# First modulation of a two-layer mixer kernel: eight tiles of two k instead of four blocks of four

## The reference

```
shift, scale, gate = split(SiLU(cond) @ w_mod[l] + b_mod[l], 3)       # w_mod[l]: 2048 x 6144
xn   = rmsnorm(x, norm_w) * (1 + scale) + shift
proj = xn @ w_in[l]                                                   # 2048 -> 6176 columns
```

## Time and profile before

| | us |
|---|---|
| three executions | 2139.41, 2141.55, 2141.57 |
| the profiled execution | 2140.41 |
| its span, first to last instruction | 2138.6 |
| PE busy in the span | 2103.1 |
| VectorE busy | 1447.0 |
| ScalarE busy | 644.0 |

### The profile page before, as it was taken

One profiled execution on the slowest core, in us unless ns is written; L12 is line 12 of the kernel. 1 busy time (PEld: TensorE's weight loads), 2 busy tenths in 40 slices (PEclk: granted clock), 3 DMA queues, 4 the chain that ended last, 5 costly groups with the idle time before them and its releaser, 6 DMA issues.

```text
span 2138.6 us, 34996 instructions
## 1 busy us (share of the span) xinstructions
PE 2103.1 (98%) x13797; PEld 1894.9 (89%) x13797; DVE 1447.0 (68%) x2819; ACT 644.0 (30%) x1092; POOL 178.5 (8%) x118
## 2 busy tenths in 40 slices
PE   5999999999999999999999999999999999999998
PEld 4788887888999999999998888888799999999998
DVE  5869899999666656775465454566666566677654
ACT  4232221321333324442142222232133333353312
POOL 0000000000000000533310000000000000043321
PEclk9999999999999999999999999999999999999999
DMA  9989787675323324554435546454333233366443
GB/s 368 387 298 324 224 280 239 224 236 173 115 91 103 106 75 153 181 200 149 120 118 175 158 145 204 133 152 153 113 123 106 75 98 106 93 214 202 155 122 143
DMA packets 357333, 365.42 MB, mean 171 GB/s; under 512 B 17670, under 2 KB 264156, under 8 KB 356572
## 3 DMA queue, kind: packets, MB, share of 16 engines
q1 hardware_dynamic: 328528, 320.67, 46.8%
q10 hardware_dynamic: 28684, 43.09, 5.4%
HBM read 304.98 MB, written 58.72 MB: 170 GB/s over the span
## 4 chain that ended last, share of the span: by engine, by line
PE 95%; DMA 1%; DVE 1%; issue 1%; ACT 1%; ACTq 0%; SPq 0%; DVEq 0%
PE psP L885 31%; PE psP L959 20%; PE psP L980 11%; PE psT L897 8%; PE psO L1187 6%; PE psT L1187 4%; PE psO L1162 3%; PE psP L1116 3%; PE psT L1127 2%; PE psO L927 1%; PE psT L802 1%; PE psO L998 1%; PE psP L1199 1%; PE psP L914 0%; DMA wmod<-in_w_mod_dram 0%
## 5 line engine op out<-in xcount | busy, mean ns | idle before, releaser
L1883 DVE SCALAR_TENSOR_TENSOR macc<-mraw,cond,macc 128x384 f32<-128x384 f32 (+1 forms) x960 | 389.0, 476 | 0.0
L885 PE MATMUL psP<-x_high,high 128*128 128x512 f32 x852 | 337.2, 396 | 0.0
L885 PE MATMUL psP<-x_low,high 128*128 128x512 f32 x852 | 331.9, 390 | 0.0
L885 PE MATMUL psP<-x_high,low 128*128 128x512 f32 x852 | 331.7, 389 | 0.0
L1377 ACT ACTIVATE high<-raw 128x1024 fp32r<-128x1024 f32 x128 | 135.4, 1059 | 602.6 <-PE psT L897 494.9
L959 PE MATMUL psP<-x_high,high 128*128 128x320 f32 x1024 | 242.8, 318 | 0.0
L959 PE MATMUL psP<-x_high,low 128*128 128x320 f32 x1024 | 233.4, 309 | 0.0
L959 PE MATMUL psP<-x_low,high 128*128 128x320 f32 x1024 | 232.9, 309 | 0.0
L1901 DVE TENSOR_TENSOR low<-raw,high 128x1024 fp32r<-128x1024 f32 x128 | 156.4, 1223 | 71.3 <-ACT high L1377 71.3
L885 PEld LDWEIGHTS psP<-x_high,high 128*128 128x128 f32 x852 | 159.9, 188 | 39.7 <-issue 6.7
L885 PEld LDWEIGHTS psP<-x_low,high 128*128 128x128 f32 x852 | 159.9, 188 | 33.9
(11 more groups left out here) (332 smaller groups left out, 3784.3 us busy)
## 6 DMA issues: line engine op xcount, KB each, us to landing
raw<-in_w_in_dram SPq DMA_DIRECT2D x132, 512.0 KB, 5.9
wmod<-in_w_mod_dram SPq DMA_DIRECT2D x32, 1024.0 KB, 9.1
mraw<-in_w_mod_dram SPq DMA_DIRECT2D x64, 512.0 KB, 4.4
mraw<-in_w_mod_dram SPq DMA_DIRECT2D x32, 1024.0 KB, 7.1
raw<-in_w_in_dram SPq DMA_DIRECT2D x32, 1024.0 KB, 5.7
raw<-in_w_out_dram SPq DMA_DIRECT2D x64, 512.0 KB, 4.1
old<-x_scratch SPq DMA_DIRECT2D x64, 320.0 KB, 3.0
xf<-proj_scratch SPq DMA_DIRECT2D x48, 320.0 KB, 3.7
```

The lines of the kernel that those rows point to most:

```text
L885: mm = pe.matmul(latent_ps[m], own, moved, start=(k == 0 and w is whole and x is x_high), stop=(k == KT - 1 and x is x_low))
L1883: m = dve.scalar_tensor_tensor(acc[:, v, 0:width], mraw[hf][:, k, 0:width], c, acc[:, v, 0:width], ALU.mult, ALU.add)
```

## The change

- A modulation tile now holds shift and scale of the same two k: two times 256 columns of w_mod, each quarter loaded by two transfers of 512 KB. Eight tiles (`BLOCKS`), each followed by its two k of x. From the third tile on VectorE sums one quarter of each tile.
- The first 8 chunks are 768 columns wide (`WIDE_T`): the group's four tiles and the two extra tiles in one transfer, in two double-width slots. The order of PE within a tile is four latent pieces, two extra pieces, the prompt piece (`wide_piece`), with the next tile's quarters between them (`quarters_after`).
- x is turned by token tiles, four k to a PSUM bank, waiting for pairs of token tiles; the vector rows come after. All 20 copies are done before VectorE goes on to the statistics. The 1/rms is spread by five matmuls of x_rs with the identity.
- VectorE scales four k, takes the first chunk's low half, and scales the other 12 k after the low parts of the first tile.
- ScalarE writes x_high itself and then the same value again to `stage`; VectorE only subtracts. Latent tokens of both k come first, then context tokens.
- In SyncE's program chunks 8 and 9 follow directly on the last tile. Chunks 10 and 11 take the slots of chunk 7.

In layer 1 the semaphore counts change, the order doesn't.

```diff
+BLOCKS = MOD_CHUNKS
+BLOCK_K = KT // BLOCKS
+MOD_W = BLOCK_K * P
+QUARTER_K = KT // 4
...
+WIDE_T = GROUP_T + EXTRA_T
+WIDE_SLOTS = 2
+X_UNITS = TT * 4
+SCALED_FIRST = 2 * BLOCK_K
...
+def quarters_after(t):
+    if t == 0:
+        return {GROUP_T: (0, 1, 2), GROUP_T + 1: (3,)}
+    return {2: (1,), GROUP_T: (2,), GROUP_T + 1: (3,)}
...
+SUMMED_Q = 1
...
 def slot_user(l, n):
-    if n < RING:
-        return n - EXTRA_SLOT if l == 0 and n >= EXTRA_SLOT else None
-    if l == 0 and n < CHUNKS:
-        return n - EXTRA_SLOT
+    if wide(l, n):
+        return n - WIDE_SLOTS if n >= WIDE_SLOTS else None
     if l == 0 and n < CHUNKS + RING:
-        return [m for m in range(CHUNKS) if chunk_slot(0, m) == n % RING][-1] if n % RING < EXTRA_SLOT else "extra"
-    return n - RING
+        return CHUNKS - WIDE_SLOTS + (n - CHUNKS) // 2
+    return n - RING if n >= RING else None
...
+            def mod_block(t, q):
+                sp.wait_ge(s[f"wmod_used{q}"], t + SEED)
+                for h in range(2):
+                    sp.dma_start(wmod[q][:, :, h * MOD_W:(h + 1) * MOD_W],
+                                 wm[:, q * QUARTER_K:(q + 1) * QUARTER_K, h * D + t * MOD_W:h * D + (t + 1) * MOD_W])\
                         .then_inc(s[f"wmod_in{q}"], 16)
...
+            for t in range(BLOCKS):
+                for q in range(3):
+                    mod_block(t, q)
+                front_chunk(0, t)
+                mod_block(t, 3)
+            for n in range(CHUNKS, CHUNKS + WIDE_SLOTS):
+                front_chunk(0, n)
...
+            for u in range(X_UNITS):
+                i, q = u // 4, u % 4
+                if q == 0 and i % 2 == 0:
+                    pe.wait_ge(s[f"x_in{i // 2}"], 16 * min(2, TT - i))
+                if u >= len(start_banks):
+                    pe.wait_ge(s["x_taken"], u - len(start_banks) + 1)
+                for k in range(4):
+                    mm = pe.transpose(start_banks[u % len(start_banks)][:, k * P:(k + 1) * P],
+                                      xtok[:, i, (4 * q + k) * P:(4 * q + k + 1) * P], ident[:])
+                mm.then_inc(s["embed_turned"], 1)
...
+            mod_quarter(0, 0)
+            mod_quarter(0, 1)
+            pe.wait_ge(s["stat_rs"], 3)
+            for i in range(TT):
+                mm = pe.matmul(rstd_ps[:, i * P:(i + 1) * P], x_rs[:, i:i + 1].to_broadcast([P, P]), ident[:],
+                               start=True, stop=True)
+            mm.then_inc(s["stat_summed"], 1)
+            mod_quarter(0, 2)
+            mod_quarter(0, 3)
...
+            def wide_piece(t, i):
+                if i < GROUP_T:
+                    front_piece(0, t, i)
+                elif i < WIDE_T:
+                    extra_piece(t, i - GROUP_T)
                 else:
-                    extra_piece(j, i - BLOCK_C * PIECES)
+                    front_piece(0, t, GROUP_T)
...
+                    pe.wait_ge(s["x_taken"], X_UNITS)
+                    first_pieces(0, range(GROUP_T))
+                    for t in range(BLOCKS):
+                        for i in range(GROUP_T if t == 0 else 0, WIDE_T + 1):
+                            for q in quarters_after(t).get(i, ()) if t + 1 < BLOCKS else ():
+                                mod_quarter(t + 1, q)
+                            wide_piece(t, i)
...
-            act.wait_ge(s["x_in"], 16 * TT)
             for i in range(TT):
+                if i % 2 == 0:
+                    act.wait_ge(s[f"x_in{i // 2}"], 16 * min(2, TT - i))
                 act.activation(ytok[:, i, :], xtok[:, i, :], ACT.Square, accum_out=x_sq[:, i:i + 1]).then_inc(s["x_squared"], 1)
             ln_exp(x_var[:], x_tmp[:], x_r0[:], "stat_var", 1, "stat_exp")
+            act.wait_ge(s["rows_turned"], 1 + DEPTH)
+            for l in range(DEPTH):
+                act.activation(vecs[:, l, :], rows_ps[l], ACT.Copy).then_inc(s["head_ready"], 1)
...
-                if user == "extra":
-                    act.wait_ge(s["latent_done"], GROUP_T + EXTRA_T)
-                elif user is not None:
+                if user is not None:
...
+                    for t in range(BLOCKS):
+                        cast_chunk(t)
+                        act.wait_ge(s["mod_ready"], t + 1)
+                        act.wait_ge(s["scaled"], (t + 1) * BLOCK_K)
+                        for v, part in ((0, slice(0, DEC)), (1, slice(DEC, TOK))):
+                            for k in range(t * BLOCK_K, (t + 1) * BLOCK_K):
+                                shift, factor = mod[:, k, v:v + 1], mod_a[:, k, v:v + 1]
+                                act.activation(x_high[:, k, part], x_hat[:, k, part], ACT.Identity, bias=shift, scale=factor)\
+                                    .then_inc(s["x_high"], 1)
+                                if t > 0:
+                                    act.wait_ge(s[("x_split", "x_prompt")[v]], k - BLOCK_K + 1)
+                                act.activation(stage[k % 2][:, part], x_hat[:, k, part], ACT.Identity, bias=shift, scale=factor)\
+                                    .then_inc(s["shifted"], 1)
...
+            for u in range(X_UNITS):
+                i, q = u // 4, u % 4
+                dve.wait_ge(s["embed_turned"], u + 1)
+                dve.tensor_copy(xf[:, 4 * q:4 * q + 4, i * P:(i + 1) * P],
+                                start_banks[u % len(start_banks)].rearrange("p (a t) -> p a t", t=P)).then_inc(s["x_taken"], 1)
+            dve.wait_ge(s["x_squared"], TT)
+            dve.tensor_scalar(x_var[:], x_sq[:], 1.0 / D, EPS, ALU.mult, ALU.add).then_inc(s["stat_var"], 1)
+            refine(x_rs[:], x_var[:], x_r0[:], x_tmp[:], "stat_exp", 1, "stat_rs", 0).then_inc(s["stat_rs"], 1)
...
+                def first_low(k, v):
+                    part = (slice(0, DEC), slice(DEC, TOK))[v]
+                    dve.wait_ge(s["x_high"], x_turn(k, v) + 1)
+                    dve.wait_ge(s["shifted"], x_turn(k, v) + 1)
+                    dve.tensor_tensor(x_low[:, k, part], stage[k % 2][:, part], x_high[:, k, part].bitcast(F32),
+                                      ALU.subtract).then_inc(s[("x_split", "x_prompt")[v]], 1)
...
+                    for k in range(SCALED_FIRST):
+                        scale_x(k)
+                    chunk_low(0)
                     dve.wait_ge(s["head_ready"], 2 + DEPTH)
...
+                    for t in range(BLOCKS):
+                        flip(t)
+                        dve.wait_ge(s["mod_turned"], t + 1)
+                        first = t * BLOCK_K
+                        mod_sum([(slice(first, first + BLOCK_K), flipped(t)[:, 0:BLOCK_K]),
+                                 (slice(KT + first, KT + first + BLOCK_K), flipped(t)[:, BLOCK_K:])], 2 * t + 2, first, BLOCK_K)
+                        for v in range(2):
+                            for k in range(first, first + BLOCK_K):
+                                first_low(k, v)
+                        for k in range(SCALED_FIRST, KT) if t == 0 else ():
+                            scale_x(k)
+                        if t + 1 < BLOCKS:
+                            if vector_sums(t + 1, 0):
+                                early_sums(t + 1)
+                            chunk_low(t + 1)
```

More of the change, by code:

```diff
@@ L82, with wide @@
 MOD_CHUNKS = 2 * D // MOD_N
[L83 to L90, removed]
-PIECES = GROUP_T + 1
[L95 to L106, removed]
+BLOCKS = MOD_CHUNKS
+BLOCK_K = KT // BLOCKS
+MOD_W = BLOCK_K * P
+QUARTER_K = KT // 4
+assert BLOCK_K == CHUNK_K and CHUNKS == BLOCKS and 2 * MOD_W == MOD_N
+PIECES = GROUP_T + 1
+EXTRA_T = 2
+WIDE_T = GROUP_T + EXTRA_T
[7 more added lines that the diff above has]
+SUMMED_Q = 1
+EARLY0 = (BLOCKS - 2) * SUMMED_Q * QUARTER_K
+EARLY1 = EARLY0 - (BLOCKS - 2) * SUMMED_Q
+EXTRA_FILLS = [CHUNKS // WIDE_SLOTS - CHUNKS // RING, -CHUNKS // RING] * 2
 FLIP = 32
+def wide(l, n):
+    return l == 0 and n < CHUNKS
 def chunk_slot(l, n):
-    return n % EXTRA_SLOT if l == 0 and n < CHUNKS else n % RING
+    return n % WIDE_SLOTS * 2 if wide(l, n) else n % RING
 def chunk_fills(l, n):
-    if l == 0 and n < CHUNKS:
-        return n // EXTRA_SLOT + 1
+    if wide(l, n):
+        return n // WIDE_SLOTS + 1
     slot = n % RING
@@ L502, in front_chunk @@
                 first, k = FRONT[n // CHUNKS][0], n % CHUNKS * CHUNK_K
-                user = slot_user(l, n)
-                if user is None:
+                user, width = slot_user(l, n), WIDE_T * P if wide(l, n) else GROUP_N
+                if user is not None:
+                    sp.wait_ge(s["chunk_split"], split_turn(l, user) + 1)
+                elif l > 0:
                     sp.wait_ge(s[f"split{n // 2}"], l * per_layer + SEED)
[L506 to L509, removed]
                 sp.dma_start(ring(raw, l, n), io["w_in"][l].rearrange("(k p) n -> p k n", p=P)
[L511 to L524, removed]
-                    front_chunk(0, BLOCK_C * j)
-                else:
-                    mod_block(2 * j + 1, range(SUMMED_Q))
```

(30 more changed lines are left out.)

203 lines of the change are left out of this document (52 added, 151 removed).

## The result

The changed kernel takes **2154.29 us** (median of 4 runs, 2152.48 to 2155.39), the kernel before 2140.48 beside it (4 runs, 2138.24 to 2141.57): ratio 1.0065, 95% interval 1.0048 to 1.0082. It is slower by 13.8 us, where the sum of the forecast had 7.8. The forecast was 2149, in a range of 2139 to 2154: the direction and the places were right, the time is 0.3 us above the range.

What follows compares the result with a forecast made beforehand. TensorE was taken to bound the kernel; start, tiles and hand-over put chunk 8 at 155.6 against 147.8 us, +7.8 on 2140.4 giving 2148.2, and with 1.1 to the median 2149, range 2139 to 2154.

Steps and rivals of the forecast that it cites:

- What bounds it: Whole kernel: TensorE bounds it, its stream closed after 150 us, so the first modulation's gain or loss reaches the end whole.
- Start: Before tile 0's x: first transpose at 10.5 us, first x matmul at 34.4, 12 us earlier than 46.5.
- VectorE in tile 0: After tile 0's low parts: 12 scalings take 8.9 us and hold tile 1's flip until 49.0.
- Each tile: Modulation tiles: 14.85 us flip to flip, with 1.0 us idle PE as ScalarE makes each x twice (bounds 0 and 1.5).
- Transfers: Weight loads of the tiles: 13.5 us per tile at 369 GB/s, refill of slot 0 covered by 1.7 us.
- rival (d): Transfers bind in the tiles: at 327 GB/s a tile takes 15.2 us, time 2153; chance 0.08.
- The hand-over: Start of chunk 8: PE idles 4.0 us because ScalarE's cast of chunk 10 precedes the latent banks (bounds 0 and 7).
- The clock: New idle places at tile 1's flip and stage end: half clock might cost up to 1.9 us each, left outside the sum.
- rival (c): The clock falls in the new gaps: two falls cost 3.8 more, 2153; at every tile's gap 2160; chance 0.10.
- The sum: Up to chunk 8: start at 155.6 us against 147.8, so 7.8 us slower.

Runs made afterwards that it cites:

- busy_start: three_and_order plus 18 added 128-column identity matmuls, products unused, in PE's gaps before and around tile 0's last quarter: 2134.89 us, ratio 0.9979 to the kernel before.
- spread_scaling: Changed kernel with VectorE scaling two k behind each tile's sums instead of twelve ahead of tile 1: 2153.04 us, ratio 1.0067 to the kernel before.
- earlier_quarters: Changed kernel with the second and third quarter that PE adds in each tile one piece earlier: 2151.54 us, ratio 1.0061 to the kernel before.
- order_alone: Changed kernel with SyncE refilling w_mod's slot 1 ahead of slot 0 from the fourth tile on: 2153.96 us, ratio 1.0067 to the kernel before.
- order_quarters: earlier_quarters plus SyncE refilling w_mod's slot 1 ahead of slot 0 from the fourth tile on: 2147.09 us, ratio 1.0034 to the kernel before.
- banks_first: Changed kernel with ScalarE emptying the first group's four latent banks ahead of the cast of chunk 10: 2147.06 us, ratio 1.0039 to the kernel before.
- before_prompt_last: Kernel before, with only the last block's prompt piece moved behind the extra tiles' 24 matmuls: 2148.55 us, ratio 1.0047 to the kernel before.
- long_rows: earlier_quarters with w_mod read in 2 KB rows instead of 1 KB, transfers still 512 KB, output differs: 2150.85 us, ratio 1.0060 to the kernel before.
- three_and_order: Changed kernel with banks_first, earlier_quarters and spread_scaling together, plus w_mod's slot 1 refilled ahead of slot 0 from the fourth tile: 2138.29 us, ratio 0.9996.

## Why the prediction was wrong, and what of it held

*What bounds it.* Right. Behind 165.31 us the stream stays closed (longest wait 0.5, in the second layer as before), and the offset of chunk 9, 13.4, is the time lost, within 0.4 us, in the medians. (The experiments do not all agree so well, as said above their table, so the 0.4 is in part luck.)

*Start.* 10.82 for 10.5; 18 copies at 0.61 each for 0.6. Two terms were too small. The copies ended 1.1 late. And from the refinement (26.45) to the first scaling (30.02) it is 3.6 us where the sum had 2.1: the ten small matmuls that spread rstd take 2.06 us of it, in a stretch where the granted clock is falling (0.71 in 28 to 36), against 1.40 in busy_start, where it stays 1.00. So some 0.7 of the missing 1.5 is the clock, and the rest was counted too low at any clock. Variance and root were 0.4 faster. Together the first x matmul is 2.0 late and flip 1 1.7 late. A clock kept up would not have brought the first x matmul forward by itself: in busy_start the copies end later, and it comes at 36.61. What it cost is in the 24 first matmuls: 7.9 us, for 7 in the sum and 5.7 in busy_start.

*VectorE in tile 0.* Right in size: the 12 scalings take 8.82 us (forecast 8.9). That they alone hold tile 1 was half right: PE's last quarter of tile 1 was done at 49.6, not 46.7, and undoing the scalings gave 0.8 us (spread_scaling).

*Each tile.* Right: 14.95 for 14.85, two waits per tile, 0.9 us for 1.0. The reason held too: earlier_quarters removed those waits. One part of the working is off without effect: eight sums 0.66 apart would take 5.4 us, not 4.9.

*Transfers.* Right that they are covered: order_alone changes nothing. The rate of 369 GB/s was not reached in the kernel after (320 GB/s in 60 to 100 us, against 395), because tiles asked for no more; once earlier quarters and the order let them, 366 to 374 were (order_quarters, 80 to 120 us). These are transfers of 512 KB for w_mod and 768 KB for w_in, several of them queued at a time. The rule of the Trainium skill, "DMA: Bandwidth & Descriptors", section "Bandwidth", that asks for 1 MiB to get 75% of peak, is not borne out by these runs: 75% of the 435 GB/s that the page gives would be 326. Two prices in the prediction do not follow from their own tiles: six of 15.2 us from the flip at 49.0 end at 140.2, 2.1 behind the forecast's 138.1, where rival (d) has 3.9 more, and six of 15.3, by the page's rule, are 2.7 more, not 4.

*The hand-over.* Right: 4.0 us for 4.0, by the mechanism named. banks_first and before_prompt_last show it from both sides.

*The clock.* **This is the step that failed.** I put it down as rival (c) with a chance of 0.10 and up to 1.9 us for each of two falls. Measured: no fall at tile 1, where PE stood for 1.3 and 0.4 us (clock 1.00 in 49 to 53); a fall at the hand-over, worth 3.06, which the sum had put at nothing; and two stretches at half clock at the start, over the small matmuls and over the first x matmuls. The price of 1.9 was read from a single fall of the kernel before (4.58 for 2.72), in which the clock fell 0.7 us after the start of the 12 matmuls and rose again within them. spread_scaling has the same 4.58 behind a wait of 4.0, and the kernel after 5.46, with 7.14 for the whole chunk: one row of such a stretch is not its bound. A fall at the hand-over belonged in the sum, since the kernel before has one behind a wait of 3.4 us and the forecast's own gap was 4.0, and the upper bound should have been a whole chunk at half rate, 4.08 lost. That rival (c) names 2153, close to the 2154.3 measured, is luck: it has two falls of 1.9, of which one did not come and the other cost 3.1.

*The sum.* 7.8 forecast, + 1.7 start, + 0.9 tiles and last tile, + 3.1 clock = 13.5, against 13.4 in the trace. The 2149 was counted from a median of 2141.55 for the kernel before; with the fourth run it is 2140.48, so the number was 1.1 nearer to the result than the sum behind it.

The stretch at half clock behind a like wait is 6.8 us long in some kernels (after, before_prompt_last, earlier_quarters, order_quarters) and 3.4 in others (spread_scaling, long_rows, order_alone). The traces order them by the moment of the fall. One stretch of the kernel after, in which PE is idle to its end, and the same one of spread_scaling, in which PE restarts at 157.26:

```profile
156.00:158.00 2.00, 0.00 (x0) 0.00 (x0) 0.58 (x1) 1.17 (x2) 0.00 (x0) 0.83 1.08 426
```

```profile
156.00:158.00 2.00, 0.74 (x2) 0.65 (x3) 0.00 (x0) 1.02 (x3) 0.00 (x0) 0.87 1.05 425
```

A mean of 0.83 is 0.7 us at half clock, one of 0.87 is 0.5. So in the first the clock fell at 157.3, 0.9 us before PE restarted, in the second at 157.5, 0.2 us after. In the four kernels with 6.8 it fell 0.9 to 2.0 us before the restart; in the three with 3.4, and in the kernel before at 47.1, 0.2 to 1.1 us after it. This is an order in eight traces, not an experiment: no edit moved the fall by itself, and what sets its moment stays open. So does whether a shorter gap is harmless: the wait of 3.4 us ahead of the first x matmul has a fall in the kernel before, and that of 3.5 in before_prompt_last has none (1.00 from 40 to 53 us).

## What to carry to other kernels

When the order of pieces on the critical engine changes, look at who waits for the last of them, and at what is queued behind that waiter: here one prompt piece moved to the end, and a cast that needs it stood in front of the bank copies (7 us of 13). All seven unfilled gaps at the hand-over, 4.0 to 4.9 us on TensorE, cost their length and then a slow stretch behind it; if such a gap can't go, matmuls whose products nobody reads were worth their place in it, at a sparse start too. Loads into buffers that are used once per tile should be asked for in the order in which they are freed; here that edit was worth nothing alone (order_alone) and 0.85 us a tile once the wait that covered it was gone (order_quarters).

## What the runs showed of the hardware

At the start of three_and_order PE is busy for 1.83 us of 24 to 28, in narrow matmuls, at a clock of 1.00; from 28.5 the clock is down, 0.53 in 28 to 36 us and 0.50 in 36 to 42 us, through the first 512-column matmuls too; 18 matmuls of 128 columns in the pauses kept it at 1.00 and gave 3.4 us. 13 of them in the gap of 4.0 us gave 2.7.

The stretch at half clock behind a gap of 4.0 to 4.9 us was 3.4 or 6.8 us long, and cost 1.9, or 2.5 to 3.1: short where the clock fell after PE had restarted, long where it fell before. The Trainium skill, "TensorE: Matmul & The Clock Gate", part 1, says that the number of slow matmuls at a start differs between runs of one kernel and is not to be fitted; these traces agree as to the scatter, between kernels.

A queue of 512 KB transfers with rows of 1 KB reached 353 to 374 GB/s in 60 to 120 us when it was not held (order_quarters), and 322 to 351 when one request stood at a buffer in use (earlier_quarters).
